# Six products of a plain feed-forward column held back to stand ahead of the next column's seventh product

## What is computed

```python
def swiglu(x, w_in, w_out):
    gu = x @ w_in
    g, u = gu[..., :D_FF], gu[..., D_FF:]
    return (jax.nn.silu(g) * u) @ w_out
...
        x = layer_norm(ALPHA * x + 0.5 * swiglu(x, ffn_w_in[l, 0], ffn_w_out[l, 0]), ln_g[l, 0], ln_b[l, 0])
```

## Time and profile before

| | |
|---|---|
| time before, median of 3 | 3126.02 us (3125.79 to 3129.47) |
| the profiled execution: time, span | 3143.1 us, 3141.3 us |
| TensorE busy (matmul) | 3101.0 us, 99% of the span |
| VectorE busy | 2282.1 us, 73% |
| ScalarE busy | 1553.6 us, 49% |
| GpSimd busy | 137.9 us, 4% |
| granted TensorE clock | 1.00 |

### The profile page before, as it was taken

How to read it: one execution, slowest core, us unless ns; L and a number is a source line. 1 busy time by engine, 2 the same in 40 slices (tenths; PEclk the granted TensorE clock), 3 DMA queues, 4 the chain that set the end, 5 groups by cost and what they waited for, 6 DMA issues and landing times.

```text
span 3141.3 us, 58924 instructions
## 1 busy us (share of the span) xinstructions
PE 3101.0 (99%) x24062; PEld 2835.5 (90%) x24062; DVE 2282.1 (73%) x3483; ACT 1553.6 (49%) x2615; POOL 137.9 (4%) x144
## 2 busy tenths in 40 slices
PE   9999999999999999999999999999999999999999
PEld 9998999899989998888998788889998888889987
DVE  7878644777878877557888677658877676668884
ACT  5555344355534563563555445454554455545552
POOL 0000111100010000101000100000000000000000
PEclk9999999999999999999999999999999999999999
DMA  5434222233333433212343331122434221123432
GB/s 189 134 133 141 87 86 74 84 132 135 118 121 112 143 133 127 77 55 71 136 146 115 129 106 64 35 75 101 141 132 140 96 82 62 36 97 125 142 118 94
DMA packets 107117, 339.59 MB, mean 108 GB/s; under 512 B 11553, under 2 KB 16929, under 8 KB 106849
## 3 DMA queue, kind: packets, MB, share of 16 engines
q1 hardware_dynamic: 106848, 335.83, 31.3%
HBM read 333.55 MB, written 2.23 MB: 107 GB/s over the span
## 4 chain that ended last, share of the span: by engine, by line
PE 92%; DVE 5%; ACT 2%; issue 1%; DMA 0%; SPq 0%; POOL 0%; ACTq 0%; DVEq 0%; POOLq 0%
PE ps L881 12%; PE ps L883 12%; PE ps L882 12%; PE ps L935 5%; PE ps L934 5%; PE ps L933 5%; PE ps L263 4%; PE ps L265 4%; PE ps L264 4%; PE ps L947 2%; PE ps L948 2%; PE ps L946 2%; PE ps L2623 1%; PE ps L399 1%; PE ps L401 1%; PE ps L400 1%
## 5 line engine op out<-in xcount | busy, mean ns | idle before, releaser
L881 PE MATMUL ps<-tz,whi 128*128 128x256 f32 x1824 | 507.9, 278 | 3.4 <-ACT tmp L1368 3.4
L883 PE MATMUL ps<-tz,wlo 128*128 128x256 f32 x1824 | 507.5, 278 | 0.0
L882 PE MATMUL ps<-tz,whi 128*128 128x256 f32 x1824 | 507.5, 278 | 0.0
L241 DVE TENSOR_TENSOR wlo<-raw,whi 128x1024 fp32r<-128x1024 f32 x259 | 314.3, 1226 | 227.9 <-ACT whi L229 226.7
L883 PE MATMUL ps<-xx,wlo 128*128 128x256 f32 x1368 | 380.6, 278 | 0.0
L882 PE MATMUL ps<-xx,whi 128*128 128x256 f32 x1368 | 380.6, 278 | 0.0
L881 PE MATMUL ps<-xx,whi 128*128 128x256 f32 x1368 | 380.6, 278 | 0.0
L229 ACT ACTIVATE whi<-raw 128x1024 fp32r<-128x1024 f32 x259 | 270.9, 1055 | 209.3 <-PE ps L935 105.1
L263 PE MATMUL ps<-xx,whi 128*128 128x256 f32 x1232 | 355.5, 289 | 13.3 <-DVE xx L329 7.1
L881 PEld LDWEIGHTS ps<-tz,whi 128*128 128x128 f32 x1824 | 342.7, 188 | 4.4 <-issue 4.4
L882 PEld LDWEIGHTS ps<-tz,whi 128*128 128x128 f32 x1824 | 345.1, 189 | 0.0
(11 more groups left out here) (395 smaller groups left out, 7163.9 us busy)
## 6 DMA issues: line engine op xcount, KB each, us to landing
raw<-in_w SPq DMA_DIRECT2D x535, 512.0 KB, 4.2
fb<-in_w SPq DMA_DIRECT2D x114, 256.0 KB, 2.6
rows<-in_row SPq DMA_DIRECT2D x15, 512.0 KB, 5.1
fb<-in_w SPq DMA_DIRECT2D x6, 512.0 KB, 3.3
es<-in_w SPq DMA_DIRECT2D x6, 512.0 KB, 4.6
xr<-in_xt SPq DMA_DIRECT2D x4, 512.0 KB, 6.5
xr<-in_x SPq DMA_DIRECT2D x1, 2048.0 KB, 7.9
mn<-bounds SPq DMA_DIRECT2D x8, 256.0 KB, 4.6
```

Source lines behind the costliest of these rows:

```text
L241: v.tensor_tensor(self.wlo[self.slot(u)][:, :], self.raw[u % NRAW][:, :], f32(self.whi[self.slot(u)][:, :]), SUB).then_inc(*self.up("wlo", u))
L881: t.matmul(out, fh[:, sl], xh[:, k, :], start=first and k == 0, stop=False, skip_group_check=not first)
L882: t.matmul(out, fh[:, sl], xl[:, k, :], start=False, stop=False, skip_group_check=not first)
L883: ins = t.matmul(out, fl[:, sl], xh[:, k, :], start=False, stop=k == 3, skip_group_check=not first)
```

## The change

Six matmuls of column 2, those of block k = 3 (`HELD`) of the up half (i = 1), are left out of the plain loop and issued in column 3 between products 6 and 7, behind column 3's wait for `tl 3`. They keep their bank and their operands. Two signals follow them: the loop's last matmul now raises a mark `most`, for which ACT's `high_a(3, 3)` waits before it overwrites the second half of the weight slot, and `unit u0 + 5`, for which `gate_v(v, 2)` and `high_a(4, 3)` wait, is raised by the last held matmul. DVE's `gate_v(v, 2)` is moved: from ahead of column 3's DVE work to behind `sum_v(v, 4, 3)`, which is directly ahead of `low_v(v, 4, 0)` and `low_v(v, 4, 1)`. This is so in all six feed-forward networks. The number of instructions is the same on each engine.

```diff
+HELD = 3
...
@@ seven_t
         else:
             t.wait_ge(*c.at("tl", s, 3))
+        if not more:
+            u = self.u0 + 2 * FIRST7 - 1
+            c.halves(t, self.bank(FIRST7 - 1, 1), u, HELD, HELD, False, True).then_inc(*c.up("gemm", "unit", u))
         t.wait_ge(*c.at("flo", s, j, 3))
         t.wait_ge(*c.at("u2c", s, j))
         self.product(t, j, 7)
@@ tensor
-                    ins = c.halves(t, self.bank(j, i), u + i, k, k, k == 0, k == KD - 1)
+                    if (j, k, i) == (FIRST7 - 1, HELD, 1):
+                        continue
+                    held = (j, i) == (FIRST7 - 1, 1)
+                    ins = c.halves(t, self.bank(j, i), u + i, k, k, k == 0, k == KD - 1 and not held)
                     if k == KD - 1:
-                        ins.then_inc(*c.up("gemm", "unit", u + i))
+                        ins.then_inc(*c.up("gemm", *(("most", s) if held else ("unit", u + i))))
@@ high_a
-        if j == FIRST7 or r == 3 and j == FIRST7 + 1:
+        if j == FIRST7 and r == 3:
+            a.wait_ge(*c.at("gemm", "most", s))
+        elif j == FIRST7 or r == 3 and j == FIRST7 + 1:
             a.wait_ge(*c.at("gemm", "unit", self.u0 + 2 * FIRST7 - NW + r))
@@ vector
         self.tl_v(v, 3)
         self.tl_v(v, 4)
-        self.gate_v(v, 2)
         for j in range(FIRST7, KF):
...
             if j > FIRST7:
                 self.g2_v(v, j - 1)
+            else:
+                self.gate_v(v, FIRST7 - 1)
```

## The result

The changed kernel takes 3141.32 us (median of 20 executions, 3125.82 to 3149.78), the kernel before 3127.8 us (20, 3125.39 to 3134.72): 0.4% slower, ratio 1.0037 (95% interval 1.0027 to 1.0046). I had forecast 3126.8, with 3113 to 3136 as the range.

The account below looks back on a forecast made before the run. PE, busy 99% of the span, was taken as the bound. Shorter wait at product 7 and new wait at column 4 summed to +0.7 us, pace at no net change: 3126.02 + 0.7 = 3126.8 us, range 3113 to 3136.

Parts of the forecast that it names:

- The old wait shrinks from 0.80 to 0.12 us: At product 7 of column 3, PE's wait for ACT's copy was to shrink so, gaining 4.2 us over six networks.
- A new wait takes its place at column 4, because the gate holds the low part: Column 4's first matmul was to wait about 0.8 us for DVE's low part; both waits together, +0.7 us.
- Nothing behind it: Behind column 4's start, DVE's later work, up to 0.45 us late, was costed at nothing, at most 2.7 us in all.
- The pace is drawn anew at a restart and holds to the next: PE's 113 or 118 ns per matmul changes at a standstill, then holds; slow columns cost 6.8 us per network.
- how the numbers follow: Part weighing the paces of columns 4 to 21: 0.35 for no part or unchanged, else drawn with 0.4 for slow.
- no net change: Case of as many networks at 118 ns after as before, columns 4 to 21: 3126.8 us, chance 0.44 including filled gap.
- slower by pace: Rival: networks go slow at column 4's restart, 6.7 us each, 3133.5 for one, 3140.3 for two; chance 0.32.
- the pace plays no part in the measured times, or comes back as it was: Rival on the pace of columns 4 to 21: the first forecast, 3126.8 us, stands; chance 0.35.
- faster by pace: Rival: slow networks turn fast at column 4's restart, 3113.4 for two (0.14), 3120.0 for one net (0.09).
- Networks that go together: At column 4's restart, networks 1 and 2, then 3, 5 and 6, then 4 alone were to draw as groups.
- That the second restart alone sets the pace of columns 4 to 21: Of standstills at product 7 (0.12 us) and column 4 (0.8 us), the latter sets the pace; 6.7 us per slowed network.

Follow-up runs that it names:

- e3: Changed kernel with the gate of column 2 behind column 4's low part and twelve matmuls held instead of six: 3152.19 us, ratio 1.0022 to before.
- e9: e3 again, on the same chip as the changed kernel: 3145.23 us, ratio 1.0023 to before.
- e5: The changed kernel again, unedited, beside new executions of before: 3138.19 us against 3130.0, ratio 1.0024.
- e10: The changed kernel, unedited, in the third set beside before: 3142.6 us against 3140.97, ratio 1.0012.
- e11: Changed kernel with twelve matmuls held instead of six, gate still ahead of column 4's low part: 3136.9 us, ratio 0.9992 to before.
- e14: e11 again on another chip: 3130.89 us against before's 3130.5, ratio 1.0005.
- e1: Changed kernel with the gate of column 2 moved behind column 4's first low part: 3144.86 us against before's 3143.09, ratio 1.0012.
- e8: e1 again, beside the changed kernel on one chip: 3165.23 us against before's 3140.97, ratio 1.0083.
- e13: e12 with the last extra addition one column shorter from each network to the next (512 to 507): 3140.42 us, ratio 1.0041 to before.
- e4: Kernel before with four extra DVE additions ahead of column 4's low part, nothing held back: 3135.49 us against before's 3143.09, ratio 0.9986.
- e7: e4 with five extra DVE additions instead of four: 3143.82 us, ratio 1.004 to before.
- e12: e4 again on another chip: 3142.75 us against before's 3130.5, ratio 1.0044.

## Why the prediction was wrong

- *The old wait shrinks from 0.80 to 0.12 us*: right, 0.13.
- *A new wait takes its place at column 4, because the gate holds the low part*: right, at its place, six times. Its size was 0.1 too large: PE's matmul follows DVE's end by 0.05 us here (48.52 + 1.22 = 49.74, L902 at 49.79) and not by the 0.15 of the earlier trace rows, but its second follows 0.22 later, not 0.19. The sum of the waits was +0.7 us and measures +0.4.
- *Nothing behind it*: right; no wait at product 5 or anywhere later in column 4.
- *The pace is drawn anew at a restart and holds to the next*: right. e3 and e9 show the other side: without a restart it is carried.
- *The step that failed* is the pace, in the part on how the numbers follow. My sum carries it at nothing (no net change), and it measures about 13 us, two networks of 6.7: the rival "slower by pace" had 3140.3 for two, and the time is 3141.3. I gave 0.35 to "the pace plays no part in the measured times, or comes back as it was", and took the two networks at 118 ns of the profile as the state from which a draw would go up or down. The profiled execution was 15 us above the median. At the median of before pace is worth 10 us by the account above, and a profile without a network at 118 ns has 9.4 of it; from there a draw can only lose. I had the number in hand (17.1 us between the profile and the median) and set it aside. With it, and nothing else changed, "faster by pace" had no place, and "slower by pace" came to 0.65 x (1 - 0.6 x 0.6 x 0.6) = 0.51 instead of 0.33: a little likelier than no change. That it was two networks and not one or none, no step of mine would have told.
- *Networks that go together*: wrong. In e5 and e10 networks with equal sequences left at different paces, and the executions of the changed kernel lie at every number of steps from none to three.
- *That the second restart alone sets the pace of columns 4 to 21*: so it looks in the profiles. In the changed kernel, e5 and e10 five networks ran columns 5 to 21 at 118 ns, and in all five product 7 had run at 113, so that L902's restart set it. Yet the short wait at product 7 can't be left out of the account for that: of two kernels with nearly the same wait at L902, the one with the short wait at product 7 is 5.7 us slower on one chip (e10, e11) and 7.3 us on the other (e5, e14). It isn't the pace of product 7 that is handed on; with twelve held, seven networks ran product 7 at 118 ns and six of them left L902 at 113. The kernel that has only the short wait (e1, e8) is the slowest of all on one chip (3165.2); on the other the one without any wait (e3) lies 7 us above it.

Shown: the time lost is hardly waiting (0.4 us by the timeline), and what is read from the profiles fits pace. On the chip where the changed kernel stood 8 us above before, holding twelve brings it level; on another, where it stood 1.6 above, holding twelve brings it 4 below. So much goes with product 7's short wait. Not shown is by what path, nor why the changed kernel loses more than before: in the profiles its restart at column 4 left 13 of 18 networks at 113 ns, and the full wait at product 7, as in before, left 27 of 36: about the same share. The restart at L902 lies behind product 7 in both kernels: with twelve held, L902 stands 0.85 or 0.90 us behind product 7, with six 0.75 to 0.78, so that the moment of the release differs too. What decides a draw, and why before does so well on one chip (3130) and not on two others (3141, 3143), stays open; e13 speaks weakly against single nanoseconds of release. Which chip the executions of the first result ran on isn't known to me. On one chip and side by side the change cost 8.2 us (e5) and 1.6 (e10, whose interval takes in no difference), not 13.5; were the two kernels' first executions made on different chips, part of the 13.5 would be the chips'.

No version here beats before on both chips: e11 is 4 us below it (an interval that just takes in no difference), e14 level.

## What to carry to other kernels

When a profiled execution lies well off the median, find out what it has that the median doesn't before building on it; here it was the very quantity on which the forecast hung. In a kernel whose TensorE is busy 99% of the time, read the distance between matmul starts stage by stage, ahead of and behind each standstill: a tenth of a microsecond of waiting can end in a pace that costs 6.7 us over the next 178 (e8). And a wait that is shortened but not closed may be worse than one left alone.

## What the runs showed of the hardware

The same matmuls (128x256, each with its own weight load, granted clock 1.00) run at 113.3 or at 117.8 ns from start to start, for as long as PE doesn't stand still; a standstill of 0.13 us is enough to change it, in either direction. Without one it was carried in 12 of 12 networks (e3, e9). Counted over the profiles, a network that came in at 118 ns left product 7's restart at 113 in 10 of 13 cases after the full wait of 0.8 us, and in 4 of 9 after the short one; one that came in at 113 stayed there in 17 of 23 and 21 of 27 (after the short one 18 of 18 with the gate ahead of the low part, 3 of 9 with it behind). Behind the restart at column 4 it was 113 in 13 of 18 cases in the changed kernel, 11 of 12 with twelve held, and 23 of 24 in e4, e7, e12 and e13. Each is one execution of its kernel, and those of e4, e12 and e13 are near the shortest of theirs (3134.4, 3134.1 and 3133.8, with others up to 3147, 3150 and 3148), so that 23 of 24 is probably more than their median executions would show. The Trainium skill ("TensorE: Matmul & The Clock Gate", Back-to-back issue gap) gives 262 cycles, that is 109 ns at 2.4 GHz, for 256 columns. That is its figure for a matmul by itself; for matmuls each with a weight load, as here, it has figures at 128 and 512 columns only. No long stretch here shows 109 ns: the two paces are what there is. Between the two paces seen lie up to 42 us of this kernel (51.2 in e8 against 9.4 in e4).
